# GpSimd in place of VectorE multiplies the expert one-hots with the low part of the gates

## The reference

```python
qry = (xb @ wq).reshape(blk, 8, 2, 128)
sc = einsum('thpd,hpkd->thpk', qry, subkeys)
s1, i1 = top_k(sc[:, :, 0], 16); s2, i2 = top_k(sc[:, :, 1], 16)
cand = (s1[..., :, None] + s2[..., None, :]).reshape(blk, 8, 256)
sf, ci = top_k(cand, 16)
e1 = take_along_axis(i1, ci // 16); e2 = take_along_axis(i2, ci % 16)
eid = e1 * 128 + e2; g = softmax(sf)
act = gelu(einsum('td,thkd->thk', xb, u_tab[eid]))
out = einsum('thk,thkd->td', g * act, v_tab[eid])
```

## Time and profile before

| | |
|---|---|
| median of 3 runs | 4147.03 us (4145.79 to 4180.34) |
| the profiled execution | 4188.77 us, its span 4187.1 us |
| TensorE busy | 3849.9 us, 92% |
| VectorE busy | 2661.3 us, 64% |
| ScalarE busy | 1183.9 us, 28% |
| GpSimd busy | 668.9 us, 16% |
| slots with gates (7 of the first part) | 1772.7 to 2476.0 us of the span |

### The profile page before, as it was taken

The page is one execution under the profiler, slowest core; times in us unless marked ns, Lnnn a source line. Parts: engine busy times, 40 slices in busy tenths (PEclk is TensorE's granted clock), DMA queues, the critical chain, the costliest instruction groups (busy, mean ns, idle before and its releaser), DMA issues. The chain is left out here.

```text
span 4187.1 us, 56891 instructions
## 1 busy us (share of the span) xinstructions
PE 3849.9 (92%) x21916; PEld 2042.3 (49%) x21916; DVE 2661.3 (64%) x4847; ACT 1183.9 (28%) x1705; POOL 668.9 (16%) x536
## 2 busy tenths in 40 slices
PE   5999797699789999899999996999999999998997
PEld 3676443266545544455555553444444444444443
DVE  5133212577565306899999956877778676676676
ACT  4233221244244102334333431222212222211123
POOL 0000000233002000000000003211111244444331
PEclk8999899899799999999999998999999999999999
DMA  6232554422263216999987789999999899999994
GB/s 207 95 117 80 143 153 160 149 97 85 81 218 120 86 51 187 241 265 311 300 227 233 212 233 283 255 239 248 247 251 243 228 285 271 253 261 242 262 263 122
DMA packets 975519, 837.74 MB, mean 200 GB/s; under 512 B 753747, under 2 KB 825771, under 8 KB 967852
## 3 DMA queue, kind: packets, MB, share of 16 engines
q1 hardware_dynamic: 912324, 564.93, 53.4%
q0 software_dynamic: 58960, 211.32, 15.6%
q10 hardware_dynamic: 4032, 58.72, 3.5%
HBM read 616.53 MB, written 181.85 MB: 191 GB/s over the span
## 5 line engine op out<-in xcount | busy, mean ns | idle before, releaser
L2933 PE MATMUL ex_psy<-ex_vhi,ex_wboth 128*128 128x512 f16 x3584 | 1081.4, 381 | 34.8 <-DVE ex_wboth L2792 13.7
L2901 PE MATMUL ex_psa<-h_hi,ex_uth 128*128 128x512 f16 (+1 forms) x2048 | 727.4, 355 | 53.1 <-DMA ex_utl<-ex_ulo 45.9
L2901 PE MATMUL ex_psa<-h_lo,ex_uth 128*128 128x512 f16 (+1 forms) x2048 | 727.2, 355 | 0.0
L2901 PE MATMUL ex_psa<-h_hi,ex_utl 128*128 128x512 f16 (+1 forms) x2048 | 726.6, 355 | 0.0
L2933 PE MATMUL ex_psy<-ex_vlo,ex_wboth 128*128 128x512 f16 x1792 | 682.0, 381 | 0.0
L2933 PEld LDWEIGHTS ex_psy<-ex_vhi,ex_wboth 128*128 128x128 f16 x3584 | 351.8, 98 | 466.4 <-DVE ex_wboth L2792 18.5
L2444 POOL DMA_INDIRECT ex_ug<-in_peer_u_dram,ex_idxp x128 | 159.7, 1248 | 1464.6 <-DVE ex_ug L2757 1062.9
L2753 DVE TENSOR_TENSOR ex_acc<-ex_acc,ex_psy 128x512 f32<-128x512 f32 x434 | 291.7, 681 | 148.6 <-PE ex_psy L2933 148.6
L2541 ACT ACTIVATE ex_wboth<-ex_wa 128x896 f16<-128x896 f32 x128 | 121.6, 950 | 816.8 <-DVE ex_wa L2787 816.8
L2901 PEld LDWEIGHTS ex_psa<-h_hi,ex_uth 128*128 128x128 f16 x2048 | 201.3, 98 | 240.8 <-DMA ex_utl<-ex_ulo 32.9
L2901 PEld LDWEIGHTS ex_psa<-h_hi,ex_utl 128*128 128x128 f16 x2048 | 201.4, 98 | 190.8 <-issue 6.5
(11 more groups left out here) (388 smaller groups left out, 6061.8 us busy)
## 6 DMA issues: line engine op xcount, KB each, us to landing
ex_u<-in_peer_u_dram SPq DMA_DIRECT2D x128, 512.0 KB, 6.0
ex_v<-in_peer_v_dram SPq DMA_DIRECT2D x128, 512.0 KB, 4.1
gate_all<-rt_stage ACTq DMA_DIRECT2D x28, 2048.0 KB, 7.3
ex_gate<-gate_all SPq DMA_DIRECT2D x128, 448.0 KB, 7.8
act_all<-ex_wa SPq DMA_DIRECT2D x80, 448.0 KB, 3.3
ex_wa<-act_all SPq DMA_DIRECT2D x80, 448.0 KB, 5.5
ad_w<-in_ada_w_dram SPq DMA_DIRECT2D x8, 2048.0 KB, 10.3
sh_w<-in_w_in_dram SPq DMA_DIRECT2D x10, 1024.0 KB, 8.3
```

The lines of the kernel that those rows point to most:

```text
L2901: mm = nc.tensor.matmul(ps_a[:, at:at + e - a], x[s][:, k, :], h[:, k, a:e], start=(k == 0 and j == 0), stop=(k == KD - 1 and j == 2))
L2933: mm = nc.tensor.matmul(sum_bank(q, n), w, v_[:, a * 512:(a + 1) * 512], start=(j == 0), stop=(j == len(mms) - 1))
```

## The change

GpSimd gets a loop over the 112 groups, behind its first gather of U rows and ahead of the rest of its work. It waits for the comparison of group g (`hot_eq`) and for the scatter that frees its buffer, and writes the low part of `hot_g`. VectorE keeps the high part. Both read the e2 one-hots and `pk`. TensorE's scatter waits for a new semaphore `hot_low` besides `hot`. VectorE waits, before it overwrites `pk` with the next tile's picks, until GpSimd has done the 16 groups of the tile before.

```diff
+            def gates_of(g, part):
+                return pk[:, g % PER_TILE, part, :].rearrange("p (a b) -> p a b", b=INNER)\
+                    .unsqueeze(2).broadcast_to([P, BT // INNER, KEYS, INNER])
             @block.gpsimd
...
                 gather("peer_u", ug, u_rows, 0, dotted)
+                for g in range(GROUPS_A):
+                    pool.wait_ge(hot_eq, g + 1)
+                    if g >= 3:
+                        pool.wait_ge(scattered, g - 2)
+                    nc.gpsimd.tensor_tensor(hot_g[g % 3][:, 1], hot_e[g % 3][:, 1], gates_of(g, 3), ALU.mult).then_inc(hot_low, 1)
                 run_unrolled(half)
...
                 def picks(d):
                     dve.wait_ge(picks_tr, d + 1)
+                    if d:
+                        dve.wait_ge(hot_low, d * PER_TILE)
...
                     dve.wait_ge(hot_eq, g + 1)
-                    for c in range(2):
-                        last = V.tensor_tensor(hot_g[s][:, c], hot_e[s][:, 1],
-                                               pk[:, g % PER_TILE, 2 + c, :].rearrange("p (a b) -> p a b", b=INNER)
-                                               .unsqueeze(2).broadcast_to([P, BT // INNER, KEYS, INNER]), ALU.mult)
-                    last.then_inc(hot, 1)
+                    V.tensor_tensor(hot_g[s][:, 0], hot_e[s][:, 1], gates_of(g, 2), ALU.mult).then_inc(hot, 1)
...
                     pe.wait_ge(hot, g + 1)
+                    pe.wait_ge(hot_low, g + 1)
```

More of the change, by code:

```diff
@@ L2229, in experts @@
          "uhi", "ulo", "acted", "gelu", "w", "whi", "wlo", "vhi", "vlo", "y", "added", "ready"))
-    (sc_in, sc_free, step_s, numbers_in, numbers_out, exp_in, exp_done, routed, picks_tr, pk_step, hot_eq, hot, scattered,
+    (sc_in, sc_free, step_s, numbers_in, numbers_out, exp_in, exp_done, routed, picks_tr, pk_step, hot_eq, hot, hot_low, scattered,
      evac) = (pr.sem(f"rt_{n}") for n in (
-         "scin", "scfree", "step", "numin", "numout", "expin", "exp", "routed", "pickstr", "pkstep", "hoteq", "hot",
+         "scin", "scfree", "step", "numin", "numout", "expin", "exp", "routed", "pickstr", "pkstep", "hoteq", "hot", "hotlow",
          "scattered", "evac"))
```

## The result

The changed kernel takes 4177.95 us against 4162.76 us of the kernel before (medians of 19 runs each), a ratio of 1.0049 with a 95% interval of 1.0028 to 1.0070. The ratio is not that of the two medians: by it the change costs 20 us, 12 to 29 by its interval, while the medians are 15 us apart. Predicted was +20.5. The profiled execution took 4164.4 us (span 4162.4). It is shorter than that of before (4188.8) although the changed stretch is longer: from the last scatter to the end before took 1712 us and after 1670, and single executions of the kernel before range over 43 us.

A forecast was written before the change was run, and what follows sets the result against it. VectorE's way from picks to group 15, plus 4.8 us of TensorE, bounds each 9-block slot. Per slot 10.7 - 9.0 + 1.6 = +3.3 us, six +19.8, last slot +0.7: 4147.0 + 20.5 = 4167.5 us, range 4118 to 4240.

The forecast's parts named there:

- What bounds a slot: 9-block slots: length is VectorE's way from picks to group 15 plus 4.8 us of TensorE; floor 97.4 us.
- Who collides: VectorE instructions behind groups 6, 8, 12 to 15 wait for GpSimd; five before group 15 cost 10.7 us a slot.
- Who goes first: After each group's comparison, VectorE's high product starts 0.11 us before GpSimd's product, which waits for it.
- Rival 2: GpSimd starts before VectorE's high product, which waits about 2.3 us in every group: +163 us, 4310; chance 0.12.
- The searches are open: VectorE's one-input searches and maxima behind the other ten groups run unhindered beside GpSimd: no cost taken, 2.14 us each at most.
- Rival 3: First half: searches also held up by GpSimd, +148 us, 4296; second: product takes 3.0 us, +59, 4206; chance 0.16.
- The product's length: GpSimd's low product of 128x1024 f16 takes 2.35 us, from an f32 addition; recorded at about 2.9 with its wait.
- the price: Delay of a VectorE instruction held up behind GpSimd's product: it can go at 2.75 us, not 0.61, so 2.14 us.
- my own formula: Per 9-block slot: five delays 10.7, less VectorE's saving 9.0, plus group 15's later arrival 1.6: +3.3 us.
- rival 4: Savings and delays cancel, as with a GpSimd product of 1.8 us: nothing to be seen, 4147; chance 0.08.
- What costs nothing: Picks' new wait, V-row gather delayed from 1725.6 to about 2475 (reader at 2507.2), and TensorE's second wait: no cost.

The follow-up runs named there:

- e3: The changed kernel without any low product; TensorE's second matmul of each pair reads the high part again: 4135.64 us, ratio 0.9950 to the kernel before.
- e4: The changed kernel, but VectorE makes both products of groups 6, 8, 12, 13, 14, 15, GpSimd the low product of the other ten: 4134.89 us, ratio 0.9956.
- e6: The changed kernel, but GpSimd makes the low product of groups 6, 8, 12 to 15 only, VectorE both of the other ten: 4202.72 us, ratio 1.0108.
- e1: The changed kernel, but GpSimd's low product waits for VectorE's high product, not the comparison: slots 103.1 us against 105.6; one execution, 4198.9 us.
- e5: The changed kernel plus 32 unread matmuls ahead of the scatters of groups 14 and 15 in six tiles: 4170.52 us, ratio 1.0033.
- e7: The changed kernel, but VectorE makes both products of groups 14 and 15 of each tile: 4154.81 us, ratio 0.9995.

## Why the prediction was right, step by step

The sign and the path were right; that the sum agrees so closely is luck, as the fifth and sixth point say. The time itself, 4167.5 us, started from the 4147.0 of three executions; in 19 the kernel before has 4162.8 and the changed one 4178.0.

- *What bounds a slot* (VectorE's way from the picks to group 15, then TensorE) held for the sign and for the undisturbed slots. e3 sets the bound at 96.7 us, for which the prediction had 97.4.
- *Who collides*: the six groups named from the code are the six that are longer, no other. e4 and e6 separate them: ten groups without price, six with all of it.
- *Who goes first*: VectorE's high product, by 0.05 us where I read 0.11. Rival 2 did not come, but stood closer than told.
- *The searches are open*: shown, 285 ns beside GpSimd as before. Rival 3's first half is out. Its second half too, since the product is shorter than taken, not longer.
- *The product's length* was mis-sized: taken from the f32 row as 2.35 us, measured 1.89 by itself (e1), recorded with 2.40 where 2.9 was told. With it the price is 1.70 and not 2.14, and group 15 comes 1.2 us later and not 1.6. By my own formula a slot would then have cost 5 x 1.70 - 9.0 + 1.2 = +0.7 us, some 4 us in the six, which is nearly rival 4.
- *What was missing* are two terms. VectorE's saving in the first groups runs into ScalarE's half of the split, which stands in ScalarE's queue behind copies that wait for TensorE: 2.3 us more a slot (e6, where VectorE is never ahead, has none of it). And TensorE's longer waits at groups 14 and 15 are followed by a stretch at the lower clock: 1.6 us where it falls behind group 15. Together 8.5 - 9.0 + 1.2 + 2.3 + 1.6 = +4.6, measured +4.4 (105.6 against 101.2).
- *Slot by slot* the six went by +3.0, +5.9, +1.9, +1.1, +4.3 and +4.5 us, where +3.3 each was predicted. In the first, third and fourth the lower clock falls between groups 14 and 15, where TensorE would wait anyway: the next picks come 4.8 us after group 15 as before, and the first slot's +3.0 is the sum above without the clock. In the second, fifth and sixth they come 6.3 to 6.5 us after. Six times 3.0 and three times 1.6 make 22.8, measured 20.7; the 2 us between are mostly in the three slots with waits on data, which I can't break down. So the profile's total agrees with the forecast to 1 us because one term was too large and two were left out, which is luck; and the interval of the measured cost, 12 to 29 us, would have held other sums as well.
- *What costs nothing*: the last slot has +0.4 us, where 0.7 was predicted. The delayed gather of V rows starts at 2486.4, where 2475 was told, and VectorE's first reader of V rows at 2525.7, behind no wait.

## What to carry to other kernels

Before an elementwise step is moved from VectorE to GpSimd, list what VectorE runs in the next two microseconds. Where one of those reads two SBUF tensors, or is like the two here a conversion or a scalar operation on a uint32 tensor in SBUF (285 ns became 1983, and 219 became 1916), the move costs more than it saves (1.70 for 0.60 us). Where it is over 2 us of searches and maxima the move is free; of reads of PSUM only the earlier trace rows tells. A step can be given out group by group on that ground, and given out so (e4) it was the only form tried that made the kernel faster with both products made. And an engine relieved of work gains only up to the next queue it waits for: leave the work out once, as in e3, to see the bound.

## What the runs showed that I had not expected

- A product of two f16 tensors of 128x1024, one of them repeated, takes GpSimd 1.89 us, an f32 addition of the same size 2.35.
- GpSimd's recorded time contains its wait for VectorE: 2.40 us for 1.89 of work, with no sign of it in the row.
- TensorE's waits of 2.7 to 2.8 us at group 14 and 2.4 us at group 15, with 6 us of work between them, brought the lower clock for some microseconds in each of six slots: three times within the first wait and three times at the second. The length of a wait alone doesn't tell: before the change the clock fell once in these slots, within a wait of 2.9 us for group 6 in the fourth, and not at one as long in the third. Without the long waits, by 32 short matmuls ahead of each scatter (e5), or with waits of 1.5 and 1.3 us (e7) or 1.8 and 1.2 us (e1), the fifth and sixth slot kept the higher one. The price was 1.6 us in three of the six, more than the last wait itself had grown (2.4 for 1.3).
